# Two unused tensors ahead of and behind h's high part and remainder in SBUF

## The reference

```
for l in range(DEPTH):                                    # DEPTH = 2
    mod = c_act @ ada_w[l] + ada_b[l]
    sh_m, sc_m, g_m, sh_f, sc_f, g_f = split(mod, 6)
    h = modulate(rmsnorm(x, mix_pre_g[l]), sh_m, sc_m)
    y = mixer_sublayer(h, w_in[l], ...)                   # h @ w_in (1024 x 6816), three mixers, gates, w_out
    x = x + g_m * rmsnorm(y, mix_post_g[l])
    h = modulate(rmsnorm(x, ffn_pre_g[l]), sh_f, sc_f)
    y = conv_glu(h, ffn_w_up[l], ...)                     # h @ w_up (1024 x 5632), conv, gelu, w_down
    x = x + g_f * rmsnorm(y, ffn_post_g[l])
```

## Time and profile before

| | us |
|---|---|
| median of 3 runs | 997.23 |
| lowest, highest | 996.12, 998.87 |
| the profiled execution, its own time | 995.64 |
| its span, first to last instruction | 994.0 |
| TensorE (PE) busy | 959.8 |
| VectorE (DVE) busy | 717.7 |
| ScalarE (ACT) busy | 526.3 |
| GpSimd (POOL) busy | 43.6 |

### The profile page before, as it was taken

The page is one execution under the profiler, slowest core; times in us unless marked ns, Lnnn a source line. Parts: engine busy times, 40 slices in busy tenths (PEclk is TensorE's granted clock), DMA queues, the critical chain, the costliest instruction groups (busy, mean ns, idle before and its releaser), DMA issues.

```text
span 994.0 us, 17872 instructions
## 1 busy us (share of the span) xinstructions
PE 959.8 (97%) x6976; PEld 897.2 (90%) x6976; DVE 717.7 (72%) x958; ACT 526.3 (53%) x701; POOL 43.6 (4%) x85
## 2 busy tenths in 40 slices
PE   6899999999998999999989999999999999999997
PEld 6799989999987999999969999899999799999996
DVE  4689766676667888787776966677667689676675
ACT  4346855455446654554574475643445656554544
POOL 0000000000000100000000000000000000000000
PEclk9799999999999999999999999999999999999999
DMA  9985755556572787777636864556646557555541
GB/s 356 374 258 177 247 161 165 192 191 213 173 265 73 270 301 247 241 246 239 241 115 192 276 211 156 157 175 224 228 137 225 185 193 273 187 183 181 180 156 43
DMA packets 134138, 206.35 MB, mean 208 GB/s; under 512 B 6336, under 2 KB 104384, under 8 KB 133952
## 3 DMA queue, kind: packets, MB, share of 16 engines
q1 hardware_dynamic: 122416, 162.07, 49.9%
q0 software_dynamic: 11520, 41.95, 11.5%
q10 hardware_dynamic: 144, 1.51, 0.4%
HBM read 204.46 MB, written 1.05 MB: 207 GB/s over the span
## 4 chain that ended last, share of the span: by engine, by line
PE 88%; DVE 4%; ACT 3%; DMA 2%; SPq 1%; issue 1%; DVEq 0%; ACTq 0%
PE banks L1602 78%; DMA raw<-in_w_in 2%; PE banks L1618 1%; DVE w_lo L1039 1%; SPq L449 1%; PE banks L1888 1%; PE banks L1891 1%; PE banks L1626 1%; PE banks L1732 1%; PE banks L1714 1%; DMA raw<-in_ada_rows 1%; ACT h L597 1%; ACT w_hi L548 1%; DVE x L1129 1%; PE banks L1662 1%
## 5 line engine op out<-in xcount | busy, mean ns | idle before, releaser
L1602 PE MATMUL banks<-h_lo,w_hi 128*128 128x256 f32 x1504 | 430.5, 286 | 3.4 <-DVE h_lo L1100 3.0
L1602 PE MATMUL banks<-h_hi,w_lo 128*128 128x256 f32 x1504 | 425.5, 283 | 0.0
L1602 PE MATMUL banks<-h_hi,w_hi 128*128 128x256 f32 x1504 | 425.5, 283 | 0.0
L1602 PEld LDWEIGHTS banks<-h_lo,w_hi 128*128 128x128 f32 x1504 | 288.4, 192 | 7.1 <-DVE h_lo L1100 3.8
L1602 PEld LDWEIGHTS banks<-h_hi,w_lo 128*128 128x128 f32 x1504 | 288.5, 192 | 2.2 <-issue 1.4
L1602 PEld LDWEIGHTS banks<-h_hi,w_hi 128*128 128x128 f32 x1504 | 288.4, 192 | 0.0
L1039 DVE TENSOR_TENSOR w_lo<-raw,w_hi 128x2048 fp32r<-128x2048 f32 x82 | 187.2, 2290 | 71.0 <-ACT w_hi L548 70.8
L548 ACT ACTIVATE w_hi<-raw 128x2048 fp32r<-128x2048 f32 x82 | 156.0, 1911 | 120.1 <-PE banks L1602 99.1
L1541 DVE TENSOR_TENSOR w_lo<-raw,w_hi 128x2048 fp32r<-128x2048 f32 x56 | 128.0, 2286 | 22.6 <-ACT w_hi L925 22.6
L925 ACT ACTIVATE w_hi<-raw 128x2048 fp32r<-128x2048 f32 x56 | 107.2, 1914 | 41.8 <-PE banks L1602 41.8
L1518 DVE SCALAR_TENSOR_TENSOR EF<-banks,par,EF 128x254 f32<-128x254 f32 (+1 forms) x176 | 76.7, 477 | 49.9 <-ACT EF L906 44.5
(11 more groups left out here) (280 smaller groups left out, 1238.9 us busy)
## 6 DMA issues: line engine op xcount, KB each, us to landing
raw<-in_w_in SPq DMA_DIRECT2D x52, 1024.0 KB, 6.1
raw<-in_ffn_w_up SPq DMA_DIRECT2D x44, 1024.0 KB, 5.1
adw<-in_ada_rows POOLq DMA_DIRECT2D x80, 512.0 KB, 4.7
raw<-in_ffn_w_down SPq DMA_DIRECT2D x22, 1024.0 KB, 4.9
raw<-in_w_out SPq DMA_DIRECT2D x8, 1024.0 KB, 7.7
raw<-in_ret_wo SPq DMA_DIRECT2D x4, 1024.0 KB, 5.0
raw<-in_lru_wo SPq DMA_DIRECT2D x4, 1024.0 KB, 7.2
raw<-in_mla_wo SPq DMA_DIRECT2D x4, 1024.0 KB, 6.9
```

The lines of the kernel that those rows point to most:

```text
L1602: ins = MM(ps, lhs, rhs, start=first and n == 0, stop=last and n == 2)
```

## The change

Two tensors that nothing reads or writes are allocated, one of one word ahead of `h_hi` and one of fifteen words behind `h_lo`.

```diff
         x = sb("x", [P, TC, D])
         h32 = sb("h32", [P, DK, T])
+        sb("space_a", [P, 1])
         h_hi = sb("h_hi", [P, DK, T], F32R)
         h_lo = sb("h_lo", [P, DK, T], F32R)
+        sb("space_b", [P, 15])
         adw = sb("adw", [P, 2, D])
```

## The result

The changed kernel takes 990.38 us (median of 4, 988.19 to 990.67) against 996.7 us for the kernel before (median of 4, 996.12 to 998.87): ratio 0.9927, 95% interval 0.9909 to 0.9944. The forecast was no change; the kernel became 6.3 us quicker. The profiled execution took 988.19 us, with a span of 986.4.

What follows compares the result with a forecast made beforehand. The prediction took TensorE, busy 97% of the span, to bound the kernel. All terms were 0, so the profiled 995.64 us stayed 995.64; with the median 1.59 above, it forecast 997.2 us, range 994 to 1002.

Steps and rivals of the forecast that it cites:

- What bounds the kernel: Whole span: TensorE busy 97% of 994.0 us; 4512 L1602 products streaming h at 120 ns each take 541 us.
- Where h lands: SBUF allocation: sizes round up to 32 bytes, so h_hi and h_lo move 32 bytes, all from adw on 96.
- TensorE streaming h: L1602's 4512 products streaming h: cost taken as 0, with 1 ns each, 4.5 us, as an end either way.
- the 96 loads of h: Products with h stationary: at 2 ns per load 0.2 us, taken as 0 since a load lies under the product before it.
- VectorE, ScalarE, transfers: Other engines' work on moved tensors and transfers into them: 0; VectorE at most 0.2 us where TensorE idles, 5.7 without cover.
- Rival A: h's streams: a true 4-byte shift makes each pay for one more memory piece, 1.7 ns, 7.7 us, 1005; chance 0.03.
- Rival B: h's streams: a 4-byte shift halves TensorE's read rate, about 430 to 450 us more, 1,430 to 1,450; chance 0.01.
- Rival C: L1602's products: a start 32 bytes past a multiple of 64 costs 1 ns each, 4.5 us, 1001.7; chance 0.05.
- Rival D: h's streams: the shift gains 1 ns each, 992.7, as h's rows lie otherwise against VectorE's and ScalarE's writes; chance 0.04.

Runs made afterwards that it cites:

- the sweep: Small program of products alone, h used 0 to 496 bytes past the weights; 47 steps streaming h took 5.71 us at distance 0, 5.41 at 64.

## Why the prediction was wrong

*What bounds the kernel* held: TensorE, through thousands of L1602 products with nothing beside them. A nanosecond per product of h is 4.5 us, as the prediction said; the products lost 3.05.

*Where h lands* held to the byte: 32 and 96, not 4 and 64.

*TensorE streaming h* is the step that failed. The prediction took 0, with 1 ns as an end, from VectorE's rows (682 against 682), and wrote that "a gain has no mechanism in any row". VectorE's rows do hold after the change too, and say nothing of TensorE, which reads a stationary tile while a stream runs; the term measured −3.05 ns × 4512 = −13.8 us. It asked what a start 32 bytes past a multiple of 64 costs, and that was the wrong question: with everything moved by 32 the step stays 119.91. It is the distance from the weights that counts.

*The products that stream weights* weren't priced at all. The prediction took only the 96 loads of h, hidden under a product, at 190 against 188 ns; the 744 products past oa and ob, which moved too, are in no term. Oa's loads after the change still take 188, and yet the step of the product beside them went from 227.7 to 233.9, which costs 4.6 us. It offsets a third of what h gains, so the forecast missed by 6.3 us where its term for h alone was off by 13.8. The prediction's price of a load was right, and its inference from it wrong: a load that is hidden can lengthen the stream that hides it.

*VectorE, ScalarE, transfers* at 0 held, as far as the rows show: L1102 688, L608 627, adw's waits 3.8 instead of 4.4 us.

*Rival A* named 1005 us for a true shift of 4 bytes, and the kernel made for it took 1006.98. That is luck: its h_lo stood at 132, and with both tensors at 4 the sweep's 123.3 ns make it some 15 us, 1012, by estimate. The rule beside it, from the Trainium skill ("SBUF — State Buffer", "SBUF: two separate sides"), has a cost for each 16-byte line crossed, and so would price 4, 12 and 28 bytes alike, since each row touches 65 lines. The sweep has 123.3, 116.7 and 115.6 for them, against 120.0 at 0. The runs don't agree with the rule here. *Rival B* fell: 4 bytes cost 3.3 ns in the sweep, not 95. *Rival C* fell with the kernel in which all moved by 32. *Rival D* was right in its sign; its reason, other engines' rows, was wrong, since the steps are there with TensorE alone, and its size, 1 ns, was a third of the fact.

What stays open is the mechanism below the distance. That concurrent loads and streams disturb each other, with a period of 256 bytes, fits the runs; how memory is divided was not shown, nor what picks a pace at 64 bytes, nor why an own start of 16 bytes differs. Whether VectorE's or ScalarE's simultaneous reads shift the cycle in the full kernel was not tried.

## What to carry to other kernels

Where a run of short products bounds a kernel and each has a new stationary tile, the start of the streamed tensor relative to the stationary one (modulo 256 bytes) is a parameter to be swept, for each pair of tensors and for either one streaming; here one unused tensor gave 2.3%, and with h offset inside longer tensors it was 2.7%. Where there are two paces, one product ahead of a group can pick the other, so a sweep needs several starts for each distance. A tensor made longer to hold an offset moves the next one too: read the addresses of all of them. Any edit of the tensor list moves everything behind it, so a difference of 1% after such an edit may be nothing but this: compare TensorE's mean step between like products, and the addresses, before crediting the edit. A load that is hidden under a product isn't free for that reason alone: here its place changed the product's step.

## What the runs showed of the hardware

The step of back-to-back products of 256 fp32r columns with a new 128x128 stationary tile each lies between 113.3 and 123.3 ns at the 2.4 GHz level in the sweep, where only the distance of the two operands was changed; with 512 columns it lies between 226.7 and 235.0 ns. The two orders don't agree: 32 and 112 bytes are good when the activation streams and bad when the weights do, 192 is good or nearly so for both.

The Trainium skill ("TensorE: Matmul & The Clock Gate", "Step-by-step: what each phase is for") gives TensorE two independent read ports of SBUF, and says that "Loading the next tile's weights doesn't steal SBUF read bandwidth from the running matmul." The runs don't agree: the step beside the loads goes from 113.3 to 123.3 ns with the distance of the two operands, and after a product at distance 0 it fell from 120.0 to between 118.3 and 119.2 ns when only the loads beside that product were moved.

At 32, 188 and 192 bytes the same distance ran at two paces, 113.3 and 117.8 ns at 192, with nothing changed but the product ahead of the group and the work before it, and once steady kept its pace to the end of the group. At 64 bytes both paces appeared, in different programs.
